# Differential attention: the two maps of a head are combined before the transpose and the product with the values

## What is computed

```python
def diff_attention(q, k, v, ...):                 # 8 heads, 2 maps of 64 columns each, values of 128 columns
    q = rotary_2(rmsnorm(q, q_gain), c, s_)
    k = rotary_2(rmsnorm(k, k_gain), c, s_)
    o = causal_block_attention(q, k, v, DIFF_HEAD_DIM ** -0.5)      # softmax(q_m k_m^T) v for m = 0, 1
    lam = exp(sum(lv[0] * lv[1])) - exp(sum(lv[2] * lv[3])) + lam_init
    o = o[:, :, :, 0, :] - lam * o[:, :, :, 1, :]
    o = rmsnorm(o, out_gain) * (1.0 - lam_init)
```

## Time and profile before

| | |
|---|---|
| time, 3 runs | 2455.55, 2456.3, 2460.32 us; median 2456.3 |
| profiled execution | 2454.26 us, span 2453.0 us |
| PE busy | 2383.8 us, 97% of the span |
| DVE, ACT, POOL busy | 1522.1, 1188.9, 284.1 us |
| granted PE clock | 0.993 over the span |
| DMA | mean 168 GB/s, weight queue 52.3% of 16 engines |
| differential attention | about 1507 to 1591 us in the first mix stage, about 2046 to 2125 us in the second |

### The profile page before, as it was taken

One profiled execution on the slowest core, in us unless ns is written; L12 is line 12 of the kernel. 1 busy time (PEld: TensorE's weight loads), 2 busy tenths in 40 slices (PEclk: granted clock), 3 DMA queues, 4 the chain that ended last, 5 costly groups with the idle time before them and its releaser, 6 DMA issues.

```text
span 2453.0 us, 34976 instructions
## 1 busy us (share of the span) xinstructions
PE 2383.8 (97%) x14214; PEld 2053.0 (84%) x14214; DVE 1522.1 (62%) x2325; ACT 1188.9 (48%) x1782; POOL 284.1 (12%) x247
## 2 busy tenths in 40 slices
PE   9999999899999999999999999999999999999999
PEld 8987787689979977777899787787998877887997
DVE  6555556776556657666655677755665587656654
ACT  4444454344444445444444464554554455554543
POOL 1100010000000000000000122333100122333000
PEclk9999999999999999999999999999999999999999
DMA  8755545456556655544566654445566554445564
GB/s 228 206 196 172 162 123 150 121 154 188 183 179 182 183 190 175 169 140 154 165 181 205 192 162 148 122 128 164 180 187 216 177 169 123 122 145 163 175 187 146
DMA packets 269424, 411.69 MB, mean 168 GB/s; under 512 B 13770, under 2 KB 141658, under 8 KB 269264
## 3 DMA queue, kind: packets, MB, share of 16 engines
q1 hardware_dynamic: 262400, 389.59, 52.3%
q0 software_dynamic: 6432, 19.28, 3.0%
q10 hardware_dynamic: 432, 0.59, 0.1%
HBM read 408.31 MB, written 1.10 MB: 167 GB/s over the span
## 4 chain that ended last, share of the span: by engine, by line
PE 77%; DVE 14%; ACT 5%; issue 2%; POOL 1%; DMA 1%; SPq 0%; ACTq 0%; DVEq 0%
PE banks L1605 14%; PE banks L1607 14%; PE banks L1606 14%; PE banks L1631 10%; PE banks L1632 10%; PE banks L1640 9%; DVE w_lo L2186 3%; ACT w_hi L1884 3%; PE banks L1754 1%; PE banks L1694 1%; DVE probs L2373 1%; PE banks L1707 1%; DVE mx_merged L2861 1%; ACT probs L1992 1%; POOL stat L2873 1%
## 5 line engine op out<-in xcount | busy, mean ns | idle before, releaser
L2186 DVE TENSOR_TENSOR w_lo<-w_raw,w_hi 128x1024 fp32r<-128x1024 f32 x688 | 838.6, 1224 | 688.6 <-ACT w_hi L1884 686.8
L1884 ACT ACTIVATE w_hi<-w_raw 128x1024 fp32r<-128x1024 f32 (+2 forms) x744 | 777.2, 1049 | 572.7 <-PE banks L1607 412.1
L1631 PE MATMUL banks<-xt_hi,w_hi 128*128 128x256 f32 x1920 | 476.4, 284 | 7.1 <-ACT xt_hi L1914 3.9
L1632 PE MATMUL banks<-xt_hi,w_lo 128*128 128x256 f32 x1920 | 475.1, 284 | 0.0
L1605 PE MATMUL banks<-w_hi,xt_hi 128*128 128x512 f32 (+2 forms) x1088 | 447.2, 411 | 11.5 <-DVE w_lo L2186 3.8
L1607 PE MATMUL banks<-w_hi,xt_lo 128*128 128x512 f32 (+2 forms) x1088 | 427.6, 393 | 0.0
L1606 PE MATMUL banks<-w_lo,xt_hi 128*128 128x512 f32 (+2 forms) x1088 | 426.8, 392 | 0.0
L1631 PEld LDWEIGHTS banks<-xt_hi,w_hi 128*128 128x128 f32 x1920 | 365.1, 190 | 9.7 <-issue 6.2
L1632 PEld LDWEIGHTS banks<-xt_hi,w_lo 128*128 128x128 f32 x1920 | 364.7, 190 | 0.0
L1640 PE MATMUL banks<-xt_lo,w_hi 128*128 128x256 f32 x1920 | 270.7, 283 | 0.0
L1605 PEld LDWEIGHTS banks<-w_hi,xt_hi 128*128 128x128 f32 x1088 | 206.4, 190 | 59.1 <-DVE w_lo L2186 6.3
(11 more groups left out here) (398 smaller groups left out, 2822.7 us busy)
## 6 DMA issues: line engine op xcount, KB each, us to landing
w_raw<-in_w_mlp SPq DMA_DIRECT2D x128, 512.0 KB, 3.9
w_raw<-in_w_in SPq DMA_DIRECT2D x104, 512.0 KB, 3.7
w_raw<-in_ffn_w_gate SPq DMA_DIRECT2D x88, 512.0 KB, 4.0
w_raw<-in_ffn_w_up SPq DMA_DIRECT2D x88, 512.0 KB, 4.3
w_raw<-in_ffn_w_down SPq DMA_DIRECT2D x88, 512.0 KB, 3.6
w_raw<-in_attn_w_in SPq DMA_DIRECT2D x72, 512.0 KB, 3.8
w_raw<-in_ret_w_in SPq DMA_DIRECT2D x64, 512.0 KB, 3.8
w_raw<-in_ret_w_out SPq DMA_DIRECT2D x16, 512.0 KB, 3.6
```

Of the source, the lines that this page charges most:

```text
L1631: pe.matmul(out[f], hi[:, cols], xh, start=(c == 0), stop=False)
L1632: pe.matmul(out[f], lo[:, cols], xh, start=False, stop=False)
L1884: act.activation(k.w_hi[i % SPLIT][:, 0:m], k.raw[i % RAW][:, 0:m], ACT.Copy).then_inc(*ev.mark(k.w_hi_made, ("w_hi", i)))
L2186: dve.tensor_tensor(lo, raw, hi.bitcast(F32), ALU.subtract).then_inc(*ev.mark(k.w_lo_made, ("w_lo", i)))
```

## The change

Per head, DVE now combines the two unnormalized maps in place, as soon as both exponentials are there (`diff_combine`): two reciprocals, the factor `-lam / d1 * d0` for each row, and two multiply-adds over the probabilities (256 and 128 columns). The sign of lam is folded into its constant. PE transposes the combined map and multiplies it by the values once. ACT writes the output out of PSUM with the scale 1/d0 (`diff_out`, two instructions of 128 columns). A new generator `attention_by_pairs` sets the order: scores as before; the combination of a pair in the even step after its two, ahead of the next map's mask; its transposes in the odd step after that; its values and its output in the even step after that. One more step than before is taken per layer.

```diff
@@ -295,6 +295,7 @@
     place: int = 0
     per_bank: int = 1
     raw: object = None
+    ready: tuple = ()
     rows: object = None
     scaled: list = field(default_factory=list)
 
@@ -837,6 +838,29 @@
                 self.step("values", h)
                 if h.place == per_bank - 1:
                     done(h, i - 2 - h.place)
+            yield
+
+    def attention_by_pairs(self, heads, by_whom, ratio, done):
+
+        n = len(heads)
+        pairs = [heads[i:i + 2] for i in range(0, n, 2)]
+        for h, _ in pairs:
+            h.group, h.per_bank, h.ready = (by_whom, h.uid), 1, ("combined", h.uid)
+        for i in range(n + 3):
+            if i < n and i % 2 == 0:
+                self.step("scores_pair", heads[i], heads[i + 1])
+            if 2 <= i < n + 2 and i % 2 == 0:
+                ratio(*pairs[i // 2 - 1])
+            if i < n:
+                self.step("scores", heads[i], True)
+            if i >= 3 and i % 2 == 1:
+                h = pairs[(i - 3) // 2][0]
+                h.by = self.by_turns()
+                self.step("turn_probs", h)
+            if i >= 4 and i % 2 == 0:
+                h = pairs[i // 2 - 2][0]
+                self.step("values", h)
+                done(h)
             yield
 
 
@@ -1475,13 +1499,21 @@
                 made[kind].append(("divided", h.uid))
             return done
 
-        def diff_done(h, h0):
-            self.step("diff", h, den[:, h0:h0 + 2, :], o_diff[:, h0 // 2, :, :], lam, layer, self.stat(4))
+        diff_factors = {}
+
+        def diff_ratio(one, two):
+            at = one.uid
+            diff_factors[at] = self.stat(4), self.stat(2)
+            self.step("diff_combine", one, two, lam, layer, *diff_factors[at])
+
+        def diff_done(h):
+            n = len(made["diff"])
+            self.step("diff_out", h, diff_factors[h.uid][0], o_diff[:, n, :, :])
             made["diff"].append(("diffed", h.uid))
 
         def attend(kind, per_bank, done):
             heads = list(heads_of(kind))
-            yield from self.attention(heads, per_bank, kind + L, done, kind == "diff")
+            yield from self.attention(heads, per_bank, kind + L, done)
             got[kind, "vals"] = "vals", heads[-1].uid
 
         turned_out = set()
@@ -1489,7 +1521,9 @@
         def outputs():
             yield from need("qt", "kt", "v")
             self.share = 2
-            yield from attend("diff", 2, diff_done)
+            heads = list(heads_of("diff"))
+            yield from self.attention_by_pairs(heads, "diff" + L, diff_ratio, diff_done)
+            got["diff", "vals"] = "vals", heads[-2].uid
             yield from need("cqt")
             yield from attend("cross", 2, divided("cross", o_cross, CROSS_D, 2, 2 * DIFF_H + MLA_H))
             yield from need("mqt", "mkt")
@@ -1731,7 +1765,7 @@
         if what == "turn_probs":
             h, = of
             bank = yield from bank_for("probs_t", h.uid)
-            q.wait_ge(*(yield from ev.of("exp", h.uid)))
+            q.wait_ge(*(yield from ev.of(*h.ready or ("exp", h.uid))))
             p = k.probs.held["probs", h.uid]
             for kh in range(2):
                 for s in range(2):
@@ -2012,6 +2046,16 @@
             act.activation(pt[:, :, :, :].rearrange("p k s t -> p (k s t)")[:, 0:n], bank[:, 0:n], ACT.Copy).then_inc(
                 *ev.mark(k.act_done, ("probs_turned", h.uid), ("bank", "probs_t", h.uid)))
             give_bank("probs_t", h.uid)
+
+        if what == "diff_out":
+            h, inv, out = of
+            bank = yield from banks.of("values", *h.group)
+            q.wait_ge(*(yield from ev.of("vals", h.uid)))
+            q.wait_ge(*(yield from ev.of("den_inv", h.uid)))
+            for s in range(2):
+                names = [("diffed", h.uid), ("bank", "values", *h.group)] if s else [("diffed_part", h.uid)]
+                act.activation(out[:, s, :], bank[:, s * 2 * DIFF_D:(s + 1) * 2 * DIFF_D], ACT.Copy, scale=inv[:, s:s + 1]).then_inc(*ev.mark(k.act_done, *names))
+            give_bank("values", *h.group)
 
         if what == "keep" and of[1] == "act":
             h, _, dst, after = of
@@ -2769,7 +2813,7 @@
             q.wait_ge(*(yield from ev.of("lam_exps", layer)))
             dve.tensor_tensor(lam[:, 4:5], lam[:, 2:3], lam[:, 3:4], ALU.subtract).then_inc(*ev.mark(k.dve_done, ("lam_diff", layer)))
             q.wait_ge(*(yield from ev.of("lam_diff", layer)))
-            dve.tensor_scalar(lam[:, 5:6], lam[:, 4:5], lam_init, None, ALU.add).then_inc(*ev.mark(k.dve_done, ("lam", layer)))
+            dve.tensor_scalar(lam[:, 5:6], lam[:, 4:5], -1.0, -lam_init, ALU.mult, ALU.add).then_inc(*ev.mark(k.dve_done, ("lam", layer)))
 
         if what == "mem_rows":
             layer, half, _, sums, total, mean, _ = of
@@ -2818,28 +2862,23 @@
             dve.tensor_tensor(out, view, each, ALU.mult).then_inc(*ev.mark(k.dve_done, ("divided", h.uid), ("bank", "values", *h.group)))
             give_bank("values", *h.group)
 
-        if what == "diff":
-            h, den, out, lam, layer, inv = of
-            bank = yield from banks.of("values", *h.group)
-            rv = inv.rearrange("p (s m) -> p s m", s=2)
-            q.wait_ge(*(yield from ev.of("vals", h.uid)))
-            q.wait_ge(*(yield from ev.of("exp", h.uid)))
-            dve.reciprocal(rv, den.rearrange("p m s -> p s m")).then_inc(*ev.mark(k.dve_done, ("den_inv", h.uid)))
-            q.wait_ge(*(yield from ev.of("den_inv", h.uid)))
+        if what == "diff_combine":
+            one, two, lam, layer, inv, ratio = of
+            each = inv.rearrange("p (m s) -> p m s", m=2)
+            for h in (one, two):
+                q.wait_ge(*(yield from ev.of("exp", h.uid)))
+            dve.reciprocal(each[:, 0, :], one.den).then_inc(*ev.mark(k.dve_done, ("den_inv", one.uid)))
+            dve.reciprocal(each[:, 1, :], two.den).then_inc(*ev.mark(k.dve_done, ("den_inv", two.uid)))
             q.wait_ge(*(yield from ev.of("lam", layer)))
-            dve.tensor_scalar(rv[:, :, 1:2], rv[:, :, 1:2], lam[:, 5:6], None, ALU.mult).then_inc(*ev.mark(k.dve_done, ("den_lam", h.uid)))
-            tmp, given = yield from k.tmp.take("diff", h.uid)
-            q.wait_ge(*(yield from ev.of("den_lam", h.uid)))
-            if given:
-                q.wait_ge(*given)
-            view = bank.rearrange("p (s m d) -> p s m d", s=2, m=2)
-            tv = tmp[:, :].rearrange("p (s m d) -> p s m d", s=2, m=2)
-            each = inv.rearrange("p (s m o) -> p s m o", s=2, o=1).to_broadcast([P, 2, 2, 2 * DIFF_D])
-            dve.tensor_tensor(tv, view, each, ALU.mult).then_inc(*ev.mark(k.dve_done, ("diff_pair", h.uid), ("bank", "values", *h.group)))
-            give_bank("values", *h.group)
-            q.wait_ge(*(yield from ev.of("diff_pair", h.uid)))
-            dve.tensor_tensor(out, tv[:, :, 0, :], tv[:, :, 1, :], ALU.subtract).then_inc(*ev.mark(k.dve_done, ("diffed", h.uid)))
-            k.tmp.give(ev.at["diffed", h.uid], "diff", h.uid)
+            q.wait_ge(*(yield from ev.of("den_inv", two.uid)))
+            dve.scalar_tensor_tensor(ratio, each[:, 1, :], lam[:, 5:6], one.den, ALU.mult, ALU.mult).then_inc(*ev.mark(k.dve_done, ("den_ratio", one.uid)))
+            q.wait_ge(*(yield from ev.of("den_ratio", one.uid)))
+            first, second = (k.probs.held["probs", h.uid] for h in (one, two))
+            for s in range(2):
+                at = slice(s * SEQ, s * SEQ + one.keys(s))
+                names = [("combined", one.uid), ("combined", two.uid)] if s else [("combined_part", one.uid)]
+                dve.scalar_tensor_tensor(first[:, at], second[:, at], ratio[:, s:s + 1], first[:, at], ALU.mult, ALU.add).then_inc(*ev.mark(k.dve_done, *names))
+            k.probs.give(ev.at["combined", two.uid], "probs", two.uid)
 
         if what == "merge":
             layer, n, half, c, b, total, gate, g = of
```

## The result

The changed kernel takes 2463.12 us (median of 17 runs, 2457.95 to 2467.22), the kernel before 2457.09 (17 runs, 2453.27 to 2460.32). The ratio is 1.0024, with a 95% interval of 1.0018 to 1.0031: 6 us slower, just over the prediction's bound of 0.2%, which the interval includes. It lies within the predicted range, 6 us above the predicted time, on the side of rival 2.

A forecast was written before the change was run, and what follows sets the result against it. At times a DVE and ACT chain, later PE, sets the pace; the chain takes PE's 15.5 us saving, layers end at 0, so 2454.3 becomes about 2454.8, plus 2.0 for the median: 2457 us, range 2443 to 2469.

The forecast's parts named there:

- the prediction's bound of 0.2%: Whole kernel: a change within 4.9 us counts as the same, about what a measurement tells from no change; chance 0.38.
- rival 2: DVE's combination: POOL's split holds it up and the kernel gets slower, 2465 us with two more waits per layer; chance 0.30.
- What PE saves, 15.5 us: PE in the mix stages: 0.97 us saved per pair, 8 pairs in 2 layers, 15.5 us.
- The chain takes what PE saves: DVE and ACT chain: grows from 6.73 to 7.66 us a pair while PE falls from 8.50 to 7.53; chance 0.43.
- Some 5 us more per layer: PE's waits at values or transposes, for ACT's copy or DVE's combination: some 5 us more than before per layer.
- the 82 to 85 that were to show it: First mix stage from 1507: the stretch takes 82 to 85 us if the forecast is right.
- Parts of the combination: DVE: reciprocals 0.11 and 0.20, factor 0.26, multiply-adds 0.42 and 0.29, sum 1.28 us; two ACT outputs 0.56.
- One wait for POOL per layer: DVE's combination at maps 2 and 3, behind the rotations: one wait for POOL per layer, up to 2.1 us, in the sum.
- in a pair without preparation the combination is just through in time: Against POOL's hold-up on DVE: combination needs 1.28 us, POOL starts 1.09 after the exponential, or 1.45 with a copy ahead.
- The clock is 1.00 in all four rows, so neither the clock nor the loads matter here: PE in the mix stages before the change: clock 1.00, DMA at most 0.47, so neither was given a cost.
- Behind 1590 nothing changes: Gate tiles ahead of the first merge: PE has no gap, later heads' shift costs nothing; otherwise 2.88 us per layer.
- Half a microsecond more: Sum over two layers: 0, or half a microsecond more because the first five pairs are put at +1.

The follow-up runs named there:

- with the eight gone: Changed kernel with POOL's tile of each pair moved to the step without a combination: 2453.4 us, ratio 0.9986 to the kernel before.
- the kernel with the shorter gaps: Kernel before with PE held up inside tiles of the two MLP stages, gaps 2.5 to 3.7 and 4.3 to 5.5 us: 2533.22 us.
- the kernel with the longer ones: Kernel before with PE held up in both MLP stages, VectorE's evacuation ahead, gaps 5.4 to 6.6 and 7.8 to 9.0 us: 2585.46 us.
- Mask first: Changed kernel with the combination behind the next even map's mask on DVE instead of ahead: 2449.12 us, ratio 0.9973 to the kernel before.
- the one with all three moves: Changed kernel with combination behind the even mask, turn ahead of the odd mask and exponential, POOL's tile in the other step: 2447.74 us, ratio 0.9963.
- the kernel without multiply-adds: Changed kernel with each combination's two multiply-adds cut to multiplications of 128x2 elements, combination in its old place: 2453.72 us.

## Why the prediction was right, and where it failed

- *What PE saves, 15.5 us:* right. With it the sums above close, and 144 instructions are gone. That PE's busy time would fall by some 14 us was wrong, it fell by 3.6: a matmul at the low clock counts as busy for longer (0.63 us against 0.39 in the rows above).
- *The chain takes what PE saves:* nearly. PE's idle time grew by 7.4 and 5.5 us, 13.0 of 15.5. The place was right: PE waits at the values for ACT's copy and at the transposes for the combination. "Some 5 us more per layer" was low. Between the two matmuls that lie at about 1507 and 1591 before, 83.3 us became 85.8, just over the 82 to 85 that were to show it; in the second layer (from 2046 to 2125) 76.3 became 82.0.
- *Parts of the combination:* right. Without POOL beside it, at 1562.26, the four starts are 0.07, 0.18 and 0.26 apart and the multiply-adds take 0.75 together, 1.26 against 1.28; the two outputs on ACT take 0.35 each and start 0.25 apart, 0.60 together against 0.56:

```profile
1562.26 0.16 DVE L2870 RECIPROCAL stat<-mx_den 128x2 f32<-128x2 f32 x1
1562.33 0.15 DVE L2871 RECIPROCAL stat<-mx_den 128x2 f32<-128x2 f32 x1
1562.51 0.22 DVE L2874 SCALAR_TENSOR_TENSOR stat<-stat,lam,mx_den 128x2 f32<-128x2 f32 x1
1562.77 0.75 DVE L2880 SCALAR_TENSOR_TENSOR probs<-probs,stat,probs 128x256 f32<-128x256 f32 x2
```

- *One wait for POOL per layer:* wrong, there are four. The step that failed is "in a pair without preparation the combination is just through in time". The numbers beside it speak against it: POOL starts 1.09 us after the exponential when no copy is ahead, and the combination needs 1.28. So it was at 1516.10, where DVE had stood idle for 1.12 us with nothing ahead of the combination: POOL started 0.93 us behind the first reciprocal, 0.01 behind the second multiply-add, and still held it up. At 1572.16 POOL started 0.06 behind the second multiply-add, and that one took its usual 0.35:

```profile
1571.70 0.75 DVE L2880 SCALAR_TENSOR_TENSOR probs<-probs,stat,probs 128x256 f32<-128x256 f32 x2
1572.16 2.54 POOL L2931 TENSOR_TENSOR w_lo<-w_raw,w_hi 128x1024 fp32r<-128x1024 f32 x1 [4.71 <-ACT w_hi L1918]
```

Rival 2 was thus right in its mechanism, and the kernel came out at its sign. Its price per wait was too high: with the eight gone the time fell by 9.7 us, 1.2 each and not 2.1, and some of that is the clock, so part of each was hidden.
- *"The clock is 1.00 in all four rows, so neither the clock nor the loads matter here":* the step that failed most. The rows tell of the kernel before, and the change makes the very gaps that bring the clock down. PE stood still for 1.57 us at 1519.69 and for 2.83 at 1538.15, and behind each the granted clock is at 1.2 GHz. The sum has no term for it. The price is up to 10.2 us in the profiled execution; without it the sum of the two stretches would have been -2.6, close to the forecast of 0. That the time stayed within the range all the same is in part luck: its upper side was left open for further waits for POOL, and the clock came out of the same margin. Over the 17 runs of the changed kernel the time follows the clock: the seven with a mean clock of 0.989 or 0.990 took 2457.95 to 2462.0 us, the five at 0.984 or 0.985 2463.1 to 2467.2. The Trainium skill (page "TensorE: Matmul & The Clock Gate", "HAM oscillation — how this bites in real kernels") reckons the loss as the throttled time times the half that is missing. By that rule, the trace agrees where PE is busy at the low clock: 17.0 us of it cost 8.4 in the kernel with the shorter gaps. Where much of the low clock lies inside the gaps it does not: 58.0 us cost 14.9 in the second MLP of the kernel with the longer ones.
- *Behind 1590 nothing changes:* right. PE is busy 49.89 of 50 us there. ("Half a microsecond more" in the sum has no term of its own: +1 and -1 are 0. It is too small to matter.)
- *What no term held:* that the combination's wait for both exponentials stands ahead of the even mask was in the chain as a length. That it is a place, which could be another at no cost, was not seen. Mask first shows what it is worth: 14 us, with the gaps and the clock behind them.

How much of the 9.7 and the 14 us is gaps and how much the clock that follows them can be told only roughly. At a clock of 0.990 the differences are 4.7 and 8.3 us, so the clock has 5 and 6 of them; but only three executions of the changed kernel are at that clock, and the mean also counts what lies outside the mix stages. Open is what, beside the length of a gap, makes the clock fall. Of the kernels that compute the whole, and have no other work on PE, only the one with all three moves has no low clock in either stretch, in the one execution that was traced; its idle time is still 4.5 us a layer above that of the kernel before.

## What to carry to other kernels

When work moves from the engine that is the bound into a chain of in-order queues, ask of each new instruction what it waits for and what stands behind it; put the instruction that another engine needs soonest (here the mask) ahead of the one that waits. Then look at what POOL runs beside an instruction of DVE with two inputs in SBUF: moving its share by one step cost nothing and gave 10 us. And where the bounding engine gets gaps that it had not, price them above their length: a clock of 1.00 in the profile before holds for the gaps of that kernel (here 1.53 us at most in these stretches), and not for longer and more frequent ones.

## What the runs showed of the hardware

- On a PE that is busy otherwise the granted clock fell to 1.2 GHz at four of seven gaps of 2.5 to 3.7 us, and at all 21 of 4.3 us and more. In the changed kernel the fall came behind gaps of 1.57 and 2.83 us, in both layers, but at one of 3.2 us in one layer only.
- Two programs that do nearly the same work can differ by the clock alone: at a mean clock of 0.990 the changed kernel and the one before take the same time within 1 us, and their medians are 6 us apart.
- A multiply-add on DVE with two inputs in SBUF whose record starts at 1517.02, 0.01 us ahead of POOL's, ended behind POOL, after 2.52 us; the one at 1572.10, 0.06 us ahead of POOL, took its usual 0.35. Starts in the trace that are this close do not tell who will wait.
- An instruction on 128x2 elements waits as long as a large one: the factor, usually 0.22 us, took 1.95 beside POOL's part. One that reads a single tile, besides the factors, waits too: in the kernel without multiply-adds the multiplication of 128x2 elements at 1538.86 took 2.28 us beside POOL, where 0.22 is usual.
